# The squares of q and their sums ahead of the decay chain in the first mixer of a two-stack transformer kernel

## The reference, cut to what matters

```python
def l2_normalize(x):
    return x * lax.rsqrt(jnp.sum(x * x, axis=-1, keepdims=True) + EPS)
...
    qkv = jax.nn.silu(causal_depthwise_conv(qkv, dn_conv_w)).astype(jnp.float32)
    q = l2_normalize(qkv[..., :DN_WIDTH].reshape(Bsz, T, DN_HEADS, DN_HEAD_DIM))
    k = l2_normalize(qkv[..., DN_WIDTH:2 * DN_WIDTH].reshape(Bsz, T, DN_HEADS, DN_HEAD_DIM))
...
    g = jnp.cumsum(g.reshape(Bsz, N, C, H).transpose(0, 3, 1, 2), axis=-1)
    decay = jnp.exp(jnp.where(causal, g[..., :, None] - g[..., None, :], -jnp.inf))
```

## Time and profile before

| | us |
|---|---|
| median of 3 runs | 2012.31 (2011.21 to 2012.93) |
| the profiled execution | 2015.44 |
| its span, first to last instruction | 2013.7 |
| TensorE busy in the span | 1902.3 (94%) |
| VectorE busy | 1452.9 (72%) |
| ScalarE busy | 1001.9 (50%) |
| GpSimd busy | 234.9 (12%) |

### The profile page before, as it was taken

How to read it: one execution, slowest core, us unless ns; L and a number is a source line. 1 busy time by engine, 2 the same in 40 slices (tenths; PEclk the granted TensorE clock), 3 DMA queues, 4 the chain that set the end, 5 groups by cost and what they waited for, 6 DMA issues and landing times.

```text
span 2013.7 us, 34482 instructions
## 1 busy us (share of the span) xinstructions
PE 1902.3 (94%) x14192; PEld 1783.2 (89%) x14192; DVE 1452.9 (72%) x2203; ACT 1001.9 (50%) x1621; POOL 234.9 (12%) x182
## 2 busy tenths in 40 slices
PE   6799999979999998999899989998999899989998
PEld 5799899978989997999799979997999889989998
DVE  4565689866566987788777776998677677776555
ACT  5444544464354445545644555445545654455444
POOL 0220111111102110211100001111111100001111
PEclk9899999989999998999999999999999999999999
DMA  5223599622238973556443347894555433344452
GB/s 221 95 87 117 211 351 350 222 88 97 92 105 333 359 290 130 236 201 239 188 147 121 143 157 313 343 368 169 178 178 182 164 126 127 120 174 149 173 184 102
DMA packets 53293, 384.07 MB, mean 191 GB/s; under 512 B 5904, under 2 KB 6032, under 8 KB 6928
## 3 DMA queue, kind: packets, MB, share of 16 engines
q1 hardware_dynamic: 53136, 381.86, 50.7%
HBM read 380.79 MB, written 1.05 MB: 190 GB/s over the span
## 4 chain that ended last, share of the span: by engine, by line
PE 81%; DVE 10%; ACT 5%; issue 4%; DMA 0%; DVEq 0%; SPq 0%; ACTq 0%
PE stream L476 16%; PE stream L477 16%; PE stream L478 16%; PE works L490 5%; PE works L491 5%; PE works L492 5%; DVE w_lo L1223 2%; DVE mx L1331 2%; ACT w_hi L920 2%; PE stream L550 1%; PE stream L551 1%; PE stream L552 1%; DVE mx L1372 1%; PE works L838 1%; DVE x L1311 1%
## 5 line engine op out<-in xcount | busy, mean ns | idle before, releaser
L1223 DVE TENSOR_TENSOR w_lo<-raw,w_hi 128x1024 fp32r<-128x1024 f32 x572 | 739.7, 1310 | 180.3 <-ACT w_hi L920 154.2
L476 PE MATMUL stream<-h_hi,w_hi 128*128 128x256 f32 x2976 | 851.9, 286 | 4.9 <-DVE w_lo L1223 4.8
L477 PE MATMUL stream<-h_lo,w_hi 128*128 128x256 f32 x2976 | 844.8, 284 | 0.0
L478 PE MATMUL stream<-h_hi,w_lo 128*128 128x256 f32 x2976 | 844.6, 284 | 0.0
L920 ACT ACTIVATE w_hi<-raw 128x1024 fp32r<-128x1024 f32 x572 | 591.1, 1051 | 106.8 <-PE works L492 72.7
L476 PEld LDWEIGHTS stream<-h_hi,w_hi 128*128 128x128 f32 x2976 | 573.9, 193 | 12.0 <-issue 8.9
L477 PEld LDWEIGHTS stream<-h_lo,w_hi 128*128 128x128 f32 x2976 | 573.9, 193 | 1.8
L478 PEld LDWEIGHTS stream<-h_hi,w_lo 128*128 128x128 f32 x2976 | 573.4, 193 | 0.0
L1713 POOL TENSOR_TENSOR g_lo<-hid,g_hi 128x256 fp32r<-128x256 f32 x140 | 191.1, 1367 | 1544.9 <-ACT g_hi L950 1544.9
L1125 ACT ACTIVATE gate_t<-stream 128x256 f32<-128x256 f32 x132 | 50.7, 384 | 414.7 <-PE stream L478 406.9
L490 PE MATMUL works<-w_hi,g_hi 128*128 128x512 f32 x480 | 187.7, 391 | 3.3 <-DVE w_lo L1223 3.2
(11 more groups left out here) (454 smaller groups left out, 2199.6 us busy)
## 6 DMA issues: line engine op xcount, KB each, us to landing
raw<-w SPq DMA_DIRECT2D x294, 1024.0 KB, 4.9
mx<-w SPq DMA_DIRECT2D x64, 1024.0 KB, 7.4
par<-p_in SPq DMA_DIRECT2D x2, 1110.0 KB, 7.5
x<-x_in SPq DMA_DIRECT2D x1, 1024.0 KB, 6.8
mx<-bt_in SPq DMA_DIRECT2D x2, 512.0 KB, 6.3
out<-x SPq DMA_DIRECT2D x4, 256.0 KB, 2.6
con<-const_in SPq DMA_DIRECT2D x1, 780.0 KB, 4.8
par<-p_in SPq DMA_DIRECT2D x1, 225.0 KB, 6.9
```

The lines of the kernel that those rows point to most:

```text
L476: mm(o, hi, r_hi[:, kt, :], start=first, stop=False, skip_group_check=True)
L477: mm(o, hi, r_lo[:, kt, :], start=False, stop=False, skip_group_check=True)
L478: last = mm(o, lo, r_hi[:, kt, :], start=False, stop=end, skip_group_check=True)
L1223: v.tensor_tensor(w_lo[:, q % SLOTS, :], raw[:, chunk_of_unit[q] % RAWS, (q % 2) * UNIT:(q % 2 + 1) * UNIT], w_hi[:, q % SLOTS, :].bitcast ...
```

## The change

The steps `decay` 0 and `nsum` 0 of the table FIRST change places, in both layers:

```diff
@@ -69,7 +69,7 @@
 FIRST = (
     [("norm", 0), ("pair", 0), ("crow", 0), ("lead", 1), ("silu", 0), ("pair", 1), ("gates", 0), ("lead", 6),
-     ("silu", 1), ("pair", 6), ("gsum", 0), ("lead", 2), ("pair", 2), ("decay", 0), ("nsum", 0), ("lead", 3), ("silu", 2),
+     ("silu", 1), ("pair", 6), ("gsum", 0), ("lead", 2), ("pair", 2), ("nsum", 0), ("decay", 0), ("lead", 3), ("silu", 2),
```

## The result

| | before | changed |
|---|---|---|
| median, first comparison | 2012.49 us | 2002.75 us (2000.75 to 2004.07, 4 runs) |
| ratio | | 0.9946, 95% interval 0.9926 to 0.9966 |
| the profiled execution, span | 2013.7 us | 1999.0 us |
| mean granted clock in that span | 0.976 | 0.982 |

The change makes the kernel faster by 9.7 us in the median; 13.0 were forecast (1999.3 us, range 1995.5 to 2004.5). Three of its other six lie above the forecast range. All ten executions of the changed kernel together have a median of 2003.5.

The account below looks back on a forecast made before the run. TensorE was taken as the bound, through standing still and half clock. Gains of 7.7 us in layer 0 and 7.1 in layer 1, less 1.8 taken off, give 13.0: 2012.3 to 1999.3 us, range 1995.5 to 2004.5.

Parts of the forecast that it names:

- Step 1: ScalarE, layer 0: squares start at 53.5, the table load fits in idle time, the decay chain starts as before; cost 0.
- signs of being wrong: Wrong if L1026 starts after 57, granted clock is 0.5 beyond 66, or TensorE's waits behind L672 grow by the gain.
- Step 2: TensorE, layer 0: stands still 2.5 us instead of 7.56, L661 takes 1.7 at full clock, `lead` 3 starts at 58.2.
- The rule on the longer table switch: ScalarE's table load: the skill's page adds a drain of about 1.38 us, 2.66 in total per switch, against the change.
- step 4: TensorE: `lead` 3 and `pair` 3 lose 1.7 us to half clock, ending at 65.7; copies to 67.1, VectorE free at 67.35.
- The bound of 2.2 us: Most that an early clock fall during L661 and the small products behind could delay VectorE's line, per layer.
- Step 3: ScalarE's weights of unit 10 and VectorE's three instructions behind come 1.04 us earlier, long durations kept, ending at 67.35.
- Step 5: VectorE bounds: taps of `pair` 3 take 2.63 us, `lead` 9 starts at 71.2 instead of 78.9; gain 7.7 us, layer 0.
- TensorE alone: Rival: VectorE is free before 66, so only TensorE counts; gain 17.4 us in all, 1994.9; chance 0.07.
- The clock low for longer: Rival: clock falls near 56 and rises only after `pair` 3 at about 70.1; gain 6.4 us, 2005.9; chance 0.08.
- Given back: Rival: another wait of 7 us opens at the normalisation of k, so the time would be 2012; chance 0.05.
- Slower: Rival: waits between short work keep TensorE at 1.2 GHz up to L672; 9.8 us slower a layer, 2031.9; chance 0.03.

Follow-up runs that it names:

- weights_ahead: squares_alone, with ScalarE also making the high part of unit 10 ahead of the decay chain's table load; 1997.08 us, ratio 0.9918 to the kernel before.
- fill: The changed kernel plus 20 matmuls on TensorE in front of the sums of q, during its wait for the squares; 2005.14 us, ratio 0.9958 to the kernel before.
- no_masks: The changed kernel with GpSimd's scalings and maskings of the decays cut to one column each, output wrong; 2000.73 us, ratio 0.9938 to the kernel before.
- squares_alone: Against the kernel before, only ScalarE's squares of q go ahead of the decay chain; TensorE keeps its old order; 1997.92 us, ratio 0.9926.
- before_filled: The kernel before plus 62 matmuls on TensorE in front of the sums of q; 2008.01 us, ratio 0.9981 to the kernel before.
- filled_wide: before_filled plus one wide matmul beside each one-column product of the sums of q; one execution, 2016.25 us.
- sums_behind_lead: squares_alone with TensorE's sums of q one step later, behind `lead` 3; 1999.27 us, ratio 0.9928 to the kernel before.
- again: The changed kernel without edit, timed a second time against the kernel before in more rounds; 2004.17 us, ratio 0.9963.

## Why the prediction was right, and by how much it was off

The direction and the way the gain comes about were right: the squares fill ScalarE's idle time, and TensorE loses most of its wait and of its half clock. The size was 13.0 against 9.7, within the range; the second timing, 8.0, is within it by only 0.3 us. Point by point, on the time scale of before (1.58 us added in layer 0):

- **Step 1** held in layer 0: the squares start at 53.4, the table load is covered (1.16 us left), and L1026 is at 57.0 instead of 56.8. In layer 1 L1026 starts 10.10 us behind L1019 where it started 8.52, so 1.6 us late, which is 58.4 on this scale. A start after 57 was one of my signs of being wrong, and in layer 1 it came true; the cause is step 2. The rule on the longer table switch did not show: in weights_ahead the load has no cover at all. It starts at 55.85, right behind other work, and the activation follows at 57.15, 1.30 us later.
- **Step 2** was off by its allowance. I let the fall cost only the projection matmuls (step 4) and put 0.6 us aside for an earlier one. In layer 0 it fell at 55.0 (56.5 on this scale), just as L649 began, and TensorE's products then cost ScalarE 0.93 us. In layer 1 it fell at 430.4, under L661, so that L1356 waited 1.47 us for TensorE, and L1032 another 1.11. What I took off for this was 0.6 us a layer. Measured: 1.2 us in layer 0 (L1026 0.23 late and 0.93 behind it) and 2.7 in layer 1 (1.57 and 1.11). Fill in layer 1 is 2.2 to 2.9 us shorter with the clock up. The bound of 2.2 us was too low for layer 1.
- **Step 3** was wrong in kind. I let the masks come at the same time as before and kept VectorE's long instructions beside them. But VectorE's three instructions now met the scalings, and the maskings began 3.2 us later. L1380 took 0.68 and the second low part 1.31 us, so the three end at 66.4, not 67.35, though they began 1.3 us later than I had them.
- **Step 4** held to 0.1 us in layer 0: the taps start at 67.2. That is partly luck. They wait for ScalarE's copies of `pair` 3, not for VectorE, which is free early by the error of step 3. And `lead` 3 began 1.7 us later than forecast, but the half clock had by then fallen on L649 and was over, so the 1.7 us that I had put on the projection made up for it. In layer 1 the taps start 1.5 us later than forecast.
- **Step 5** failed: the taps of `pair` 3 at 2.63 us. They take 4.6 in layer 0 and 4.5 in layer 1, since they now meet GpSimd's two maskings, which step 3 had left where they were. This is the term that was mis-sized, by 1.9 us a layer; no_masks gives up to 1.8 of it back. The step has a slip as well: from a `pair` 3 that ends at 65.7, two more units of 2.88 us end at 71.5, not 70.3. By the terms of the forecast TensorE would then be 0.3 us behind VectorE at `lead` 9, with no new wait. It was indeed done at 71.5, and waited 1.61 us only because the taps were long. L672 came 2.2 us later than 81.4 in layer 0 and 3.6 later in layer 1, 5.8 together where I took off 1.8. 14.8 less 5.8 is the 9.0 of the stretches.
- **The rivals.** TensorE alone: no, it waits 1.6 us for VectorE, though its projection sets the start of the taps. The clock low for longer: no in layer 0, back at 58.4 on its own clock (60.0 on this scale); in layer 1 it was low from 430.4 to 437.3, and back before `pair` 3 was done. Given back: no, the waits of TensorE from L672 of layer 0 to the next L1019 are the same, 13.0 us before and 13.1 after. Slower: no. (Its six units at 24 x 0.21 us are 30.2, not 30.7, which changes nothing.)

The lesson in the sum: I moved VectorE's work by 1 us against GpSimd's, and kept each duration as it was. Both engines' durations depend on which instruction meets which, so they had to be taken again at the new place. One of the signs that I had named shows the size: at L672 the layers had gained 5.5 and 3.4 us, below the 6 to 8 written down.

## What to carry to other kernels

When an engine stands at a semaphore for work that has long had its inputs, look where the producer is in its own order; moving only that instruction into the producer's idle time (14.9 us here) was better than moving the consumer along with it (10.9 and 7.4 by the same measure), because a consumer that waits early holds back everything behind it. A duration read beside a second engine on the same memory is that pair's, not the instruction's: when the order shifts, ask which instructions meet now. And where single executions spread by 8 us with the mean clock, measure a small change by a stretch of its own stage beside the medians.

## What the hardware showed that was not expected

- **The clock fell while TensorE was busy.** In squares_alone, layer 0, granted clock by microsecond:

```profile
54.00:55.00 1.00, 1.00 (x10) 1.00 0.88 360
55.00:56.00 1.00, 1.00 (x8) 0.69 1.00 426
56.00:57.00 1.00, 1.00 (x7) 0.50 0.36 148
```

  TensorE was busy all along from the projection of `pair` 2; what it did before the fall were the small decay products and the one-column sums, L661. In the kernel before, L661 ran for 3.57 us and the clock did not rise under it. With no wait over 0.2 us in front, it fell under or behind L661 in five of eight cases (both layers of weights_ahead, one each of squares_alone, before_filled and fill). It fell in neither layer of filled_wide, with a wide matmul beside each product, nor behind L661 in either layer of sums_behind_lead, where `lead` 3 stands between the decay products and the sums. Why it falls in some layers and not in others is not shown. A busy share of 1.00 in these rows is thus no sign that the clock will stay up.
- **Who is slowed depends on which instructions of VectorE and GpSimd meet.** Beside the eight scalings VectorE loses little and GpSimd much: a low part takes 1.31 us instead of 1.22, L1380 0.68 as alone, and the scalings 5.8 to 7.5 instead of 4.67. Beside the two maskings VectorE loses most: a low part takes 2.30 us instead of 1.22, L1380 1.75 instead of 0.68, L1400 1.89 instead of 1.00, and six taps 4.5 to 4.9 instead of 2.71. Where the taps of layer 1 of `again` met only the last 1.3 us of the maskings, they took 3.81.
